# One layer of a hybrid HGRN2 and gated-delta encoder on one core: the first norm computed by feature, and two tiles with the gate columns worked off between the modulation stages

## The reference, cut to what matters

```python
mod = jax.nn.silu(c) @ w_ada[l] + b_ada[l]
sh1, sc1, g1, sh2, sc2, g2 = [m[:, None, :] for m in jnp.split(mod, N_MOD, axis=-1)]
h = rmsnorm(x, norm_mix[l]) * (1.0 + sc1) + sh1
...
proj = h @ w_in                       # 1024 features -> D_IN columns
hq, hf, hi, hog, gq, gk, gv, ga, gb, gz, gate_a, gate_b = split_cols(proj, IN_SIZES)
...
conv_out, s_conv_new = causal_conv(jnp.concatenate([gq, gk, gv], axis=-1), s_conv, conv_w)   # 4 taps, then silu
...
log_a = -jnp.exp(a_log) * jax.nn.softplus(ga + dt_bias)   # ga: 4 columns
beta = jax.nn.sigmoid(gb)                                  # gb: 4 columns
o_gdn, s_gdn_new = chunk_gated_delta(q, k, v, log_a, beta, s_gdn)
```

## Time and profile before

| | |
|---|---|
| median of 3 runs | 952.2 us (949.42 to 952.33) |
| profiled execution, its own time | 951.82 us |
| span in its trace | 950.0 us |
| mean granted TensorE clock | 0.997 |
| PE busy | 923.8 us, 97% of the span |
| DVE busy | 669.4 us, 70% |
| ACT busy | 438.2 us, 46% |

### The profile page before, as it was taken

The page is one execution under the profiler, slowest core; times in us unless marked ns, Lnnn a source line. Parts: engine busy times, 40 slices in busy tenths (PEclk is TensorE's granted clock), DMA queues, the critical chain, the costliest instruction groups (busy, mean ns, idle before and its releaser), DMA issues.

```text
span 950.0 us, 22427 instructions
## 1 busy us (share of the span) xinstructions
PE 923.8 (97%) x9425; PEld 892.8 (94%) x9425; DVE 669.4 (70%) x1254; ACT 438.2 (46%) x808; POOL 105.6 (11%) x133
## 2 busy tenths in 40 slices
PE   6999999999999999999999999999999999999997
PEld 6999888989999999999999999999999999999996
DVE  3778879866577677477766888889435899994553
ACT  6687445424223544553222257465322666662213
POOL 0110011112020110100100001122001222220000
PEclk9999999999999999999999999999999999999998
DMA  9834234444333432315643332232233343323222
GB/s 347 268 87 134 59 97 112 113 128 117 115 102 102 123 85 68 100 56 165 208 127 106 90 89 77 80 90 73 85 96 104 102 119 91 90 78 101 67 67 95
DMA packets 146175, 104.88 MB, mean 110 GB/s; under 512 B 5170, under 2 KB 139000, under 8 KB 144924
## 3 DMA queue, kind: packets, MB, share of 16 engines
q1 hardware_dynamic: 139099, 79.23, 28.6%
q0 software_dynamic: 6352, 22.00, 7.7%
q10 hardware_dynamic: 624, 2.23, 0.6%
HBM read 100.12 MB, written 3.31 MB: 109 GB/s over the span
## 4 chain that ended last, share of the span: by engine, by line
PE 48%; DVE 4%; ACT 3%; issue 2%; POOL 0%; DVEq 0%; ACTq 0%; POOLq 0%
PE G L2153 31%; PE G L2243 16%; DVE x_lo L1680 1%; DVE w_sum L1691 1%; DVE sum_lo L1700 1%; PE R L2164 0%; ACT w_hi L1306 0%; DVE w_lo L1700 0%; ACT w_hi L1219 0%; ACT b L1286 0%; ACT d_hi L1311 0%; POOL w_sum L1164 0%; PE R L2161 0%; DVE val L1711 0%; DVE w_lo L1592 0%
## 5 line engine op out<-in xcount | busy, mean ns | idle before, releaser
L2153 PE MATMUL G<-h_hi,w_hi 128*128 128x272 f32 (+1 forms) x880 | 263.7, 300 | 2.8 <-DVE ff_shift L2099 1.4
L2153 PE MATMUL G<-h_lo,w_hi 128*128 128x272 f32 (+1 forms) x880 | 253.8, 288 | 0.4 <-issue 0.4
L2153 PE MATMUL G<-h_hi,w_lo 128*128 128x272 f32 (+1 forms) x880 | 253.5, 288 | 0.1
L1592 DVE TENSOR_TENSOR w_lo<-raw,w_hi 128x1024 fp32r<-128x1024 f32 (+2 forms) x111 | 117.2, 1056 | 104.4 <-ACT w_hi L1219 103.6
L2153 PEld LDWEIGHTS G<-h_hi,w_hi 128*128 128x128 f32 x880 | 165.7, 188 | 6.2 <-DVE ff_shift L2099 1.7
L2153 PEld LDWEIGHTS G<-h_lo,w_hi 128*128 128x128 f32 x880 | 166.0, 189 | 0.6 <-issue 0.6
L2153 PEld LDWEIGHTS G<-h_hi,w_lo 128*128 128x128 f32 x880 | 165.7, 188 | 0.0
L1219 ACT ACTIVATE w_hi<-raw 128x1024 fp32r<-128x1024 f32 (+2 forms) x111 | 101.4, 914 | 90.6 <-PE G L2153 90.5
L1164 POOL TENSOR_TENSOR w_sum<-raw 128x512 f32<-128x512 f32 x36 | 50.1, 1395 | 318.3 <-DMA raw<-in_w_up 169.8
L2243 PE MATMUL G<-x_hi,sum_hi 128*128 128x272 f32 x288 | 83.7, 291 | 1.2 <-ACT partial L1322 1.1
L2243 PE MATMUL G<-x_hi,sum_lo 128*128 128x272 f32 x288 | 83.4, 290 | 0.0
(11 more groups left out here) (326 smaller groups left out, 2074.2 us busy)
## 6 DMA issues: line engine op xcount, KB each, us to landing
raw<-in_w_in SPq DMA_DIRECT2D x48, 512.0 KB, 4.1
raw<-in_w_up SPq DMA_DIRECT2D x44, 512.0 KB, 4.0
w_ada<-in_w_ada_t POOLq DMA_DIRECT2D x49, 256.0 KB, 3.2
wada<-in_w_ada_s SPq DMA_DIRECT2D x8, 1024.0 KB, 14.3
raw<-in_w_down SPq DMA_DIRECT2D x16, 320.0 KB, 3.2
raw<-in_w_out SPq DMA_DIRECT2D x8, 512.0 KB, 4.1
raw<-in_w_down SPq DMA_DIRECT2D x8, 512.0 KB, 4.1
w_ada_t<-in_w_ada_t POOLq DMA_DIRECT2D x15, 256.0 KB, 3.2
```

The source lines that it names most:

```text
L1592: dve.tensor_tensor(lo, raw[:, i % RAW, 0:job.nk, 0:job.m], hi.bitcast(F32), ALU.subtract).then_inc(w_lo_done, 1)
L2153: ins = pe.matmul(out, w, x, start=(job.first and k == 0 and p == 0), stop=(job.last and k == job.nk - 1 and p == 2))
```

## The change

The front goes by feature. `x` is loaded by feature straight into `xT` (four transfers of two chunks). `in_sq(k)` squares a chunk on ScalarE and VectorE adds it to `acc`; `in_sums` is one product with a matrix of ones; ScalarE makes `in_rn` from it (Ln, Exp), and `in_norm(k)` multiplies chunk k by it on VectorE, the chunks of a stage ahead of that stage. `x_sq`, `x_first`, `x_diag` and `xtok` go. The silu of `c_cols` becomes an Exp on ScalarE and three small VectorE instructions. `warm(b, n)` issues n matmuls of the unit matrix with itself into bank b; their results are used by nothing.

The duo is now `gk0` and `gk1`; the gate columns (loaded from a packed copy, `w_gab`) are worked off chunk by chunk as `gab_part(k)` into two banks of `R`. In each stage j the weights of job j are split ahead: `gk1`, the gate columns, `gq0`. SyncE's queue has `ones` first, then `wada` of stage 0, the weights of `gk0` and `gk1`, `wada` 1, the gate columns, `wada` 2, the weights of `gq0`, `wada` 3. Behind the duo the list is: `gab_part 6`, `gab_part 7`, `evac gk0`, `evac gagb`, `split gq1`, `evac gk1`, `job gq0`, `taps gk0`, `g_sp`, `split_hi gv0`, `g_a`, `split_lo gv0`, second half of `gq0`, `taps gk1`, `evac gq0`, `job gq1`, `taps gq0`, ... The weave with the first recurrence begins one job later, with `gq0'`.

```diff
+    do("warm", 3, 16)
+    for k in range(KD):
+        do("in_sq", k)
+        if k == 5:
+            do("vectors")
+    do("warm", 3, 12)
     do("c_cols")
+    do("in_sums")
+    do("in_norm", 0)
+    do("in_norm", 1)
     do("split", 0)
+    do("warm", 1, 10)
     do("ada_rows", 0)
     do("ada_T", 0)
+    do("warm", 1, 12)
     do("h1", 0)
     for j in range(1, STAGES):
+        do("split", (1, 2, 3)[j - 1])
+        do("in_norm", 2 * j)
+        do("in_norm", 2 * j + 1)
+        k = 2 * j - 2
+        do("duo_part", k, 0)
+        if j > 1:
+            do("gab_part", k)
         do("ada_rows", j)
+        do("duo_part", k, 1)
         do("ada_T", j)
+        do("duo_part", k + 1, 0)
+        do("duo_part", k + 1, 1)
+        if j == 1:
+            do("gab_part", 0)
+        do("gab_part", k + 1)
         do("h1", j)
...
+    for one in (gk0, gk1, gagb):
+        one()
+    evac = [s for s in plan[mark:] if s[0] == "evac"]
+    del plan[mark:]
+    plan.append(("duo", 0, 1))
+    do("gab_part", KD - 2)
+    do("gab_part", KD - 1)
+    plan.extend([evac[0], evac[2], ("split", 4), evac[1]])
+    around(gq0, [("g_sp",), ("split_hi", 5), ("g_a",), ("split_lo", 5)], [])
+    around(gq1, [("g_sq", 0, 2), ("g_scan",)], [])
...
-    weave(gdn_steps(0, ahead), parts_of(gk1, gq0, gq1, gv0, gv1, *hg_inputs("hf", 0), fine=True))
+    weave(gdn_steps(0, ahead), parts_of(gq0, gq1, gv0, gv1, *hg_inputs("hf", 0), fine=True))
...
-            while plan[at][0] not in ("job", "g_y", "g_u"):
+            while plan[at][0] not in ("half" if g == 1 else "job", "g_y", "g_u"):
...
+                elif name == "warm":
+                    if a[0] == 1:
+                        wait_bank(pe, last_bank[spot("vectors")])
+                    for _ in range(a[1]):
+                        pe.matmul(R[:, a[0], 0:P], ident, ident, start=True, stop=True, skip_group_check=True)
+                elif name == "in_sums":
+                    pe.wait_ge(ones_in, 16)
+                    pe.wait_ge(in_added, KD - 1)
+                    sums_of(n, 0, acc)
...
+                elif name == "in_norm":
+                    k = a[0]
+                    dve.wait_ge(in_rn_ready, 1)
+                    dve.tensor_tensor(xT[:, k, :], xT[:, k, :], in_rn[:, :], ALU.mult).then_inc(in_normed, 1)
```

More of the change, by code:

```diff
@@ L284, in make_plan @@
     gk0, gk1, gq0, gq1, gv0, gv1 = gdn_inputs(0)
[L285 to L290, removed]
+    mark = len(plan)
+    for one in (gk0, gk1, gagb):
[8 more added lines that the diff above has]
+    around(gq1, [("g_sq", 0, 2), ("g_scan",)], [])
+    around(gv0, [("g_sq", 0, 3), ("g_norm", 0, 2)], [("g_rows",), ("c_load",)])
+    around(gv1, [("g_sq", 0, 0), ("g_norm", 0, 3)], [("g_bcast", 0)])
     gk0, gk1, gq0, gq1, gv0, gv1 = gdn_inputs(1)
-    around(gk0, [("g_norm", 0, 1)], [])
+    around(gk0, [("g_sq", 0, 1), ("g_norm", 0, 0), ("g_rel", 0)], [])
+    around(gk1, [("g_norm", 0, 1)], [])
     ahead = [[("g_sq", 1, 2)], [("g_sq", 1, 3)], [("g_norm", 1, 2)], [("g_sq", 1, 0)], [("g_norm", 1, 3)], [],
              [("g_sq", 1, 1)], [("g_norm", 1, 0)], [("g_rel", 1)], [("g_norm", 1, 1)]]
-    weave(gdn_steps(0, ahead), parts_of(gk1, gq0, gq1, gv0, gv1, *hg_inputs("hf", 0), fine=True))
+    weave(gdn_steps(0, ahead), parts_of(gq0, gq1, gv0, gv1, *hg_inputs("hf", 0), fine=True))
     def og(n):
@@ L542, in bank_users @@
     return {
-        "vectors": ["dve"] * 2, "x_first": ["act", "dve"] if name == "x_first" and a[0] < N_CHUNK else ["act"], "sums": ["act"] * 2, "onorm": ["act"] * 2,
+        "vectors": ["dve"] * 2, "in_sums": ["act"] * 2, "gab_part": ["act"] * 2 if a[:1] == (KD - 1,) else [], "sums": ["act"] * 2, "onorm": ["act"] * 2,
         "ada_rows": ["act"], "ada_T": ["dve"], "g_rows": ["dve"], "g_norm": ["act"] * 2, "g_bcast": ["act"] * n, "g_gram": ["dve"] * n,
@@ L800, in build @@
         ident_in = sem("ident_in")
-        x_in = [sem(f"x_in{c}") for c in range(CHUNKS)]
+        x_in = [sem(f"x_in{j}") for j in range(STAGES)]
+        ones_in = sem("ones_in")
         x_again = sem("x_again")
@@ L1000, in slot_of @@
         def slot_of(g):
-            return (g + sum(groups_before[f] <= g and (run_last[f] - f + 1) % 2 for f in groups_before)) % 2
+            return (g + (g > gab_group) + sum(groups_before[f] <= g and (run_last[f] - f + 1) % 2 for f in groups_before)) % 2
         def run_before(g):
@@ L1069, in _ @@
                     sp.dma_start(wada01[:, j, v, :, :], t["w_ada_s"][j, v]).then_inc(ada_in[j], 16)
-            sp.dma_start(ones[:, :], t["all_ones"]).then_inc(const_in, 16)
+                for i in ((0, 1), (2,), (3,), ())[j]:
+                    load(i)
             sp.dma_start(sel[:, :, :], t["head_select"]).then_inc(const_in, 16)
             sp.dma_start(masks_c[:, :, :], t["level_masks_c"]).then_inc(const_in, 16)
-            sp.wait_ge(fill_done, last_bank[spot("x_first", N_CHUNK)] + 1)
+            sp.wait_ge(fill_done, last_bank[spot("vectors")] + 1)
             sp.dma_start(masks_t[:, :, :], t["level_masks_t"]).then_inc(masks_in, 16)
             for n, step in enumerate(plan):
-                if step[0] == "job" or step[0] == "duo" and step[1]:
+                if step[0] == "job" and step[1] > gab + 1 or step[0] == "duo" and step[1:] != duos[0]:
                     for i in step[1:]:
@@ L1214, in split_weights @@
                     return
-                if i in aside:
+                if aside.get(i) == "ffn":
                     act.wait_ge(job_done, i - 2)
-                elif nth_ring[i] >= 2:
+                elif i not in aside and nth_ring[i] >= 2:
                     act.wait_ge(job_done, ring[nth_ring[i] - 2] + 1)
@@ L2504, in vectors, with gate_columns @@
             np.concatenate([x["gdn_dt_bias"], x["gdn_a_log"]]).T)
+def gate_columns(w_in):
+    return w_in[0][:, COL["gagb"]:COL["gagb"] + 2 * NH].reshape(KD, P, 2 * NH).transpose(1, 0, 2)
 def by_output(w_ada):
```

198 lines of the change are left out of this document (102 added, 96 removed).

## The result

The changed kernel takes 978.62 us (median of 4 runs, 977.51 to 979.26), the kernel before beside it 952.27 us (949.42 to 952.54). The ratio is 1.0287 [1.0271, 1.0302]: 26 us slower, where +9.3 on the median was forecast and the range ended at 967. The profiled execution took 978.44 us, with a span of 976.6. The sign was right and the size was not.

What follows compares the result with a forecast made beforehand. TensorE, busy 923.8 of 950.0 us, was taken to bound the kernel. Front -0.4, chain behind the duo +7.4, weave +1.0 and clock +1.5 summed to +9.5 us, forecast 961.5, range 950.5 to 967.

Steps and rivals of the forecast that it cites:

- F: Front: time at which the first chunk of h_lo is ready after the change, forecast 22.8 us.
- the lower bound: Front: unit products at full rate from the first, in_sums waiting for the adds until 13.1, F = 21.9.
- Rival (d): Front: x late, last chunk landing at 13, sums starting at 15.4, +1.4, 963 us; chance 0.55 together with the forecast.
- Front -0.4: Opening up to the end of the gate columns: 48.0 against 48.4 us, so -0.4 (-1.7 to +1.2).
- no more than TensorE: Front stages: VectorE's work together 6.6 us per stage, against TensorE's 6.6 us.
- The two stalls of 0.35: Stages 2 and 3: two stalls before h_lo, 0.7 us together in place of 0.4.
- T0: End of the gate columns, forecast at 48.0 us (22.8 + 24.5 + 0.7), against 48.4 before.
- Rival (a): Behind the duo: evacuation hidden, both waits go; with the front's better end 949.2 us, faster; chance 0.14.
- The chain behind the duo, +7.4: Behind the duo: late slots make TensorE wait 2.8 us before gq1 and 4.3 before gv0; together +7.4 (0 to 9).
- The weave, +1.0 (0 to 4): First weave: six jobs instead of seven over the same recurrence, +1.0 us (0 to 4).
- The clock, +1.5 (0 to 5.9): Two waits behind the duo: half a clock fall, +1.5 us; two falls would be 5.9, none 0.
- rival (c): Behind the duo: clock falls in both waits, 5.9 us instead of 1.5, 966 us; chance 0.13 (up to 968).

Runs made afterwards that it cites:

- Run 5: Changed kernel with the gate columns' split one stage earlier in ScalarE's and VectorE's lists: 973.87 us, ratio 1.0246.
- run 6: Changed kernel with gk1 put back into the first weave, seven jobs instead of six: 966.80 us, ratio 1.0169.
- run 9: Run 7 plus stage 1's wada ahead of gk1's weights in SyncE's queue: 956.77 us, ratio 1.0063.
- Run 4: Changed kernel with the taps of gk0 ahead of the gate rows and those of gk1 right behind job gq0: 971.66 us, ratio 1.0214.
- Run 3: Changed kernel with VectorE's two groups of four units moved from the first weave to the second and behind: 965.48 us, ratio 1.0148.
- run 8: Kernel before the change with only the two groups of four units moved out of the first weave: 949.92 us, ratio 0.9983.
- run 1: Changed kernel with ten unit products before gq1 and sixteen before gv0, in the waits behind the duo: 977.23 us, ratio 1.0281.
- run 7: Changed kernel with three edits: groups of four moved, taps of gk0 and gk1 earlier, gate columns' split earlier: 956.06 us, ratio 1.0062.

## Why the prediction was off, step by step

**F, the first `h_lo`: right.** Forecast 22.8 with bounds 21.9 and 24.2; the first product came at 21.84, and at 21.9 to 22.9 in the experiments. It is the case of the lower bound: the first 32 unit records took 5.25 us and not 6.72, so TensorE was done with its filler first and waited 0.51 us for the adds, until 13.08 (forecast 13.1). Rival (d) did not come: the last of x was issued at 2.1 and landed 8.1 us later, at 10.2 (forecast 10.3).

**Front -0.4: measured +5.1.** Two statements failed. The first was that VectorE's load per stage, "no more than TensorE", means no stall. I summed the work in a stage and did not walk through VectorE's list: `split` of the gate columns is entry 2 and the first `gab_part` needs it in stage 1. Run 5 puts this at 3.9 us, with 1.3 of it the clock (run 6 against the changed kernel). The second was that stage 1's `wada` is there when it is wanted. The 23.3 of the earlier trace rows was its landing in the kernel before; now `gk1`'s weights stand ahead of it, TensorE wants it at 22.8, and it waits until 24.5. The two stalls of 0.35 that I put into stages 2 and 3 are there, 0.27 and 0.26. In run 9 another order of the transfers moved this wait and did not shorten it. From the first product to T0 the forecast had 25.2 us and the trace has 31.7: the two waits and the clock make 5.7 of these 6.5, and 0.8 I can't place. And the gate columns' small pieces, which I took for gone, are not: packets under 512 B are 5153 against 5170. The copy is packed at its source and not where it lands; that this is the reason is argued, no run shows it. Rival (a) also had a slip: 21.9 + 24.5 without any stall is 2.0 us ahead of 48.4, where its sum took off 2.4.

**The chain behind the duo, +7.4: right.** It measured 7.6 at `g_rows`. `gq1` came at T0 + 8.44 (forecast 8.85) and `gv0` at T0 + 18.80 (19.2). The second wait shows as 2.53 us instead of 4.3 only because `gq1`'s products ran at half clock inside it. Run 4 confirms the cause, since with the taps ahead both starts move by 2.4 and 5.4 us.

**The weave, +1.0 (0 to 4): measured 15.7.** By the table and the runs these are 0.9 up to the first `g_x`, 2.1 at the wait for `Tc`, 6.8 of clock behind it, 4.1 up to the second `v_tok,Um` (3.1 the wait for `S`, 0.5 clock), and 1.8 behind it (1.6 clock). So 8.9 are clock and 5.2 the waits. This is the step that made the forecast wrong. I read VectorE at 11.11 of 11.25 in a stretch ahead of the weave and priced the weave as one job less over the same work, by averages. What I did not look for were VectorE's long groups placed by hand, and what stands on either side of them once the jobs shift by one. Run 3 (13.2 us back), run 6 (11.2 back) and run 8 (1.6 in the kernel before) say the same thing from three sides: it is where the groups lie against the jobs, not the amount of VectorE's work. Whether the missing job did it by the phase or by the cover it gave, no run separates, since run 6 changes both. The rows speak for the phase at the first place (nine products in the gap in both kernels) and for the cover at the second (15 for 24).

**The clock, +1.5 (0 to 5.9): mis-sized, and in the wrong place.** I priced falls in the two waits behind the duo. They fell in the profile, to 0.51 and 0.57, and cost nothing (run 1), so rival (c) was right on the fall and wrong on its price. The falls that cost were at the front (1.3) and in the weave (8.9), 10.2 together. By the rule of the Trainium skill ("TensorE: Matmul & The Clock Gate", the section on what is actually happening), that a long enough idle stretch puts the throttled state back, the clock would have been 3 to 6 us. The rows agree with its direction behind the waits, in stretches that the forecast had not seen as idle, but it does not settle the falls here: the clock fell behind 1.47 us of idleness (run 6) and 1.51 (run 1), not behind the 1.69 at 22.8, and in run 9 with no idle stretch above 0.4 us in the 20 us ahead. No run shows a fall from an idle stretch that unit products had filled.

**What remains open.** The three edits together give 2.6 us less than alone, with intervals some 2 us wide. The traces show where. From T0 to the 720th product the changed kernel took 146.8 us, run 3 133.4, run 4 141.5 and run 7 128.1: the savings of runs 3 and 4 add up to 18.6 there, and run 7 has 18.7. At the front they don't: T0 is 4.4 us earlier in run 5 and 4.0 in run 7, but also 1.4 in run 4, whose profile had no fall there, so that this fall is counted twice. That the other executions were like the profiled ones is not shown. I also did not run the new front with the duo of before, so whether the front alone is worth anything is open; run 9 and the landing of `wada` only argue that it is not.

## What to carry to other kernels

When jobs are moved against a list of steps, don't price the overlap by busy shares: 11.11 of 11.25 us on VectorE did not show the 15.7 us lost here. Go through each engine's own list at every place where something long was put by hand, and ask what now stands directly ahead of it and how many products TensorE has in that gap. A weight that has landed early is worth nothing if its split stands behind a long step in the list of the engine that makes it: check each first use against the place of its producer on each engine. And here a fall of the clock cost only where TensorE itself set the pace (10.2 us in three places); ahead of a wait that other engines set, it was free, and filling the wait bought nothing.

## What I had not expected of the hardware

After the wait of 2.25 us at 143.7 the granted clock stayed at 0.50 in all of the 17 us to 161, with PE busy throughout. Behind the waits that ended at 31.8, 62, 72 and 177 (2.73, 2.23, 2.53 and 3.33 us) it was back at 1.00 within some 4 us. What followed differs: at 144 TensorE changed between products of 272 columns and many of 32 by 32, behind 62 and 72 it had `G` products alone. Whether that is the cause is open. The length is not fixed by the place either: in run 1, with the same list behind it, the fall lasted 6.8 us and a second one came at 160. Ten unit products (2.4 us of TensorE's time, most of it inside the wait) kept the clock at 1.00 there and gave back 5.9 us.

The same wait of 2.7 us for `gab_lo` came with a fall in three profiled executions (0.50 to 0.52 in the lowest window) and without in three others whose list up to there is the same (1.00 in all windows from 30 to 36). And in run 9 the clock was at 0.50 from 146.7 to 153.3, with no wait above 0.4 us in the 20 us ahead of it; run 7, with the same steps there, stayed at 1.00. Between `g_w` and the second `v_tok,Um` that made 16.4 us of 13.9. The window of run 9 around it, its mean clock 0.83:

```profile
140.00:160.00 20.00, 19.69 (x128) 18.06 (x126) 12.56 (x26) 7.72 (x20) 2.04 (x3) 0.83 0.19 55
```

So one profiled execution does not tell whether a given wait takes the clock down, and a difference of 1 to 3 us between two kernels can be a fall that the other had as well.
